# The experts' down product of a routed layer in three f32r passes, with the operand splitting on ScalarE and VectorE

## The reference, cut to what matters

```python
moe = jnp.zeros((B, T, D_MODEL), jnp.float32)
for e in range(N_EXPERTS):                      # 16
    he = jax.nn.silu(h2 @ w_gate[e]) * (h2 @ w_up[e])      # (rows, 256)
    moe = moe + combine[..., e:e + 1] * (he @ w_down[e])   # w_down[e]: (256, 1024)
x = x + moe
y = rmsnorm(x, g_final)
```

## Time and profile before

| what | value |
|---|---|
| median of 3 runs | 482.11 us (481.48 to 494.56) |
| the profiled execution, its time | 483.13 us |
| its span, first to last instruction | 481.3 us |
| PE busy | 439.2 us (91% of the span) |
| DVE busy | 231.1 us (48%) |
| ACT busy | 149.9 us (31%) |
| POOL busy | 112.3 us (23%) |
| mean granted clock of TensorE | 0.957 of full speed |

### The profile page before, as it was taken

How to read it: one execution, slowest core, us unless ns; L and a number is a source line. 1 busy time by engine, 2 the same in 40 slices (tenths; PEclk the granted TensorE clock), 3 DMA queues, 4 the chain that set the end, 5 groups by cost and what they waited for, 6 DMA issues and landing times.

```text
span 481.3 us, 7519 instructions
## 1 busy us (share of the span) xinstructions
PE 439.2 (91%) x2852; PEld 357.7 (74%) x2852; DVE 231.1 (48%) x593; ACT 149.9 (31%) x397; POOL 112.3 (23%) x200
## 2 busy tenths in 40 slices
PE   6999999999899869999997898999999999999950
PEld 3686999988678637888773785888887887878830
DVE  2754234447599866243228354222445555454450
ACT  5475223325477643321113110111221221212230
POOL 2010002000333232100003021222435444454121
PEclk9899999999999959999999798999999999999995
DMA  7851607132000597132206898889999999942100
GB/s 257 266 157 44 208 1 242 32 121 64 1 3 1 192 420 283 42 141 87 82 11 238 330 359 302 334 332 345 337 342 335 342 332 336 327 170 71 63 25 19
DMA packets 32073, 91.39 MB, mean 190 GB/s; under 512 B 11193, under 2 KB 11705, under 8 KB 27942
## 3 DMA queue, kind: packets, MB, share of 16 engines
q1 hardware_dynamic: 20790, 71.97, 41.3%
q0 software_dynamic: 11248, 18.96, 11.3%
HBM read 86.38 MB, written 26.01 MB: 234 GB/s over the span
## 4 chain that ended last, share of the span: by engine, by line
PE 56%; DMA 14%; issue 11%; POOL 7%; DVE 5%; ACT 4%; POOLq 0%; SPq 0%; DVEq 0%; ACTq 0%
PE ps L1075 12%; PE ps L749 9%; PE ps L751 8%; PE ps L750 8%; DMA out_y_sample<-region_x,lists 8%; PE ps L1083 7%; DMA region_x<-h_rows,lists 3%; PE ps L1068 2%; PE ps L870 2%; DMA region_x<-in_x_prompt 1%; POOL region_x L649 1%; PE ps L903 1%; POOL mix L649 1%; POOL out_y_prompt L654 1%; PE ps L958 1%
## 5 line engine op out<-in xcount | busy, mean ns | idle before, releaser
L1075 PEld LDWEIGHTS ps<-region_p,region_a 128*128 128x128 f32 x512 | 58.3, 192 | 3.3 <-issue 3.3
L1075 PE MATMUL ps<-region_p,region_a 128*128 128x128 f32 x512 | 58.5, 275 | 0.0
L751 PE MATMUL ps<-region_a_r,region_w_r 128*128 128x288 f32 x192 | 56.5, 294 | 0.0
L749 PE MATMUL ps<-region_a_r,ring_r 128*128 128x288 f32 x128 | 40.5, 317 | 0.0
L1914 DVE TENSOR_TENSOR region_t<-region_t,ps 128x256 f32<-128x256 f32 x16 | 6.7, 422 | 68.1 <-PE ps L1075 68.1
L750 PE MATMUL ps<-region_a_r,ring_r 128*128 128x288 f32 x128 | 37.7, 295 | 0.0
L1413 ACT ACTIVATE region_t<-ps 128x256 f32<-128x256 f32 x16 | 6.1, 384 | 98.7 <-PE ps L1075 86.5
L649 POOL DMA_INDIRECT region_x<-h_rows,lists x14 | 14.4, 1027 | 93.2 <-DVE slot_w L1909 93.2
L1403 ACT ACTIVATE region_p<-ps,gffn_sb 128x128 f32<-128x128 f32 x64 | 18.3, 368 | 57.1 <-PE ps L1068 57.1
L751 PEld LDWEIGHTS ps<-region_a_r,region_w_r 128*128 128x128 f32 x192 | 36.0, 188 | 0.0
L1075 PEld LDWEIGHTS ps<-region_p,ring 128*128 128x128 f32 x256 | 31.2, 203 | 3.1 <-DVE region_p L1813 1.7
(11 more groups left out here) (309 smaller groups left out, 902.7 us busy)
## 6 DMA issues: line engine op xcount, KB each, us to landing
region_a<-in_w_gate SPq DMA_DIRECT2D x8, 1024.0 KB
region_a<-in_w_up SPq DMA_DIRECT2D x8, 1024.0 KB
region_a<-in_w_down SPq DMA_DIRECT2D x8, 1024.0 KB
region_w<-in_w_in SPq DMA_DIRECT2D x2, 2048.0 KB, 10.3
region_w<-in_w_out SPq DMA_DIRECT2D x2, 2048.0 KB, 8.2
ring<-in_w_gate SPq DMA_DIRECT2D x4, 1024.0 KB
ring<-in_w_up SPq DMA_DIRECT2D x4, 1024.0 KB
ring<-in_w_down SPq DMA_DIRECT2D x4, 1024.0 KB
```

Source lines behind the costliest of these rows:

```text
L749: pe.matmul(out, lhs_hi, rhs_hi, start=first, stop=False)
L751: return pe.matmul(out, lhs_lo, rhs_hi, start=False, stop=last)
L1075: ins = pe.matmul(ps[:, bank, c * P:(c + 1) * P], w[:, k, c * P:(c + 1) * P], xT[:, b, k, :], start=(k == 0), stop=(k == KC - 1))
```

## The change

The down product of every expert in the main pipeline (not in the overflow branch) is split. Per expert i:

- ACT evacuates all eight transposed blocks of expert i + 1, DVE none (except for expert 0). DVE's wait for the transposes goes.
- ACT then writes the high parts of the down weights of expert i + 1, two copies of 128x1024 into `region_q` (float32r), after the weights have landed and the down product that used that half of `region_q` is done.
- DVE subtracts them from the weights in place (`wd_los`, two operations of 128x1024), after `finish` and ahead of the one-hot matrix and `add_rows`.
- `he_out` becomes three DVE operations of 128x256: the high part, the full product again, and the remainder.
- PE runs 12 float32r matmuls of 512 columns in place of 4 float32 ones, and waits for `wd_lo_ready` ahead of them and for `he_lo_ready` after the first four.

```diff
+            def down_split(u, i):
+                b = u % 2
+                for half in range(2):
+                    n = slice(half * 512, (half + 1) * 512)
+                    for c in range(FC):
+                        pe.matmul(ps[:, 4 + half, :], he_hi[:, b, c, :], wd_hi[:, b, c, n], start=(c == 0), stop=False)
+                        pe.matmul(ps[:, 4 + half, :], he_hi[:, b, c, :], wd_lo[u][:, c, n], start=False, stop=False)
+                    if half == 0:
+                        pe.wait_ge(he_lo_ready, i + 1)
+                    for c in range(FC):
+                        ins = pe.matmul(ps[:, 4 + half, :], he_lo[:, b, c, :], wd_hi[:, b, c, n], start=False, stop=(c == FC - 1))
+                    ins.then_inc(down_done, 1)
...
-                pe.wait_ge(xT_dve, i + 1)
+                if first:
+                    pe.wait_ge(xT_dve, 1)
...
-                down(u, b, down_done)
+                pe.wait_ge(wd_lo_ready, i + 1)
+                down_split(u, i)
...
+            def wd_his(i):
+                act.wait_ge(ring_loaded[i % RING], 48 * (i // RING + 1))
+                if i >= 2:
+                    act.wait_ge(down_done, 2 * i - 2)
+                elif i == 0:
+                    act.wait_ge(x2_stored, 16 * NT)
+                    act.wait_ge(h2n_ready, NT)
+                    act.wait_ge(h2_transposed, NT)
+                for c in range(FC):
+                    act.copy(wd_hi[:, i % 2, c, :], wd_sb[i % RING][:, c, :]).then_inc(wd_hi_ready, 1)
...
             ins.then_inc(xT_act, 1)
+            wd_his(0)
...
-                    for k in range(4, KC):
+                    for k in range(KC):
                         ins = rows_out((i + 1) % 2, k)
                     ins.then_inc(xT_act, 1)
+                    wd_his(i + 1)
...
-                dve.tensor_tensor(heT[:, i % 2], gact[:, i % 2],
-                                  ps[:, 3, 0:FE].rearrange("p (c s) -> p c s", c=FC), ALU.mult).then_inc(he_ready, 1)
+                b, up = i % 2, ps[:, 3, 0:FE].rearrange("p (c s) -> p c s", c=FC)
+                dve.tensor_tensor(he_hi[:, b], gact[:, b], up, ALU.mult).then_inc(he_ready, 1)
+                step(dve.tensor_tensor(gact[:, b], gact[:, b], up, ALU.mult))
+                dve.tensor_tensor(he_lo[:, b], gact[:, b], he_hi[:, b].bitcast(F32), ALU.subtract).then_inc(he_lo_ready, 1)
+
+            def wd_los(i):
+                for c in range(FC):
+                    dve.wait_ge(wd_hi_ready, FC * i + c + 1)
+                    ins = dve.tensor_tensor(wd_lo[i % RING][:, c, :], wd_sb[i % RING][:, c, :],
+                                            wd_hi[:, i % 2, c, :].bitcast(F32), ALU.subtract)
+                ins.then_inc(wd_lo_ready, 1)
...
+            wd_los(0)
             for i in range(E - 1):
                 he_out(i)
...
-                dve.wait_ge(xg_transposed, i + 2)
-                rows_out((i + 1) % 2).then_inc(xT_dve, 1)
...
                     finish(i - 1, final_ready)
+                wd_los(i + 1)
                 if i >= 1 and i + 3 < E:
                     expert_onehot(i + 3)
                 add_rows(i)
```

More of the change, by code:

```diff
@@ L135, in build @@
         wd_sb = [r[:, 2 * WB:3 * WB].rearrange("p (c n) -> p c n", c=FC) for r in ring]
-        region_q = sb("region_q", [P, 5632])
+        region_q, region_q_r = sb_both("region_q", [P, 5632])
         qT = region_q[:, 0:2304].rearrange("p (h t) -> p h t", h=H)
@@ L170, in build @@
         xT = region_p[:, :].rearrange("p (b k s) -> p b k s", b=2, k=KC)
-        region_t = sb("region_t", [P, 1536])
+        region_t, region_t_r = sb_both("region_t", [P, 1536])
         aT = region_t[:, 0:1024].rearrange("p (b k) -> p b k", b=2)
@@ L175, in build @@
         heT = region_t[:, 512:1024].rearrange("p (b c s) -> p b c s", b=2, c=FC)
+        he_hi = region_t_r[:, 512:1024].rearrange("p (b c s) -> p b c s", b=2, c=FC)
+        he_lo = region_t_r[:, 1024:1536].rearrange("p (b c s) -> p b c s", b=2, c=FC)
+        wd_hi = region_q_r[:, 0:4 * D].rearrange("p (b c n) -> p b c n", b=2, c=FC)
+        wd_lo = [r.rearrange("p (c n) -> p c n", c=FC) for r in
+                 (ring0_r[:, 2 * WB:3 * WB], region_a_r[:, 2 * WB:3 * WB], region_a_r[:, 5 * WB:6 * WB], region_w_r[:, 2 * WB:3 * WB])]
         region_x, region_x_r = sb_both("region_x", [P, 4096])
@@ L380, in build @@
         he_ready = sem("he_ready")
+        he_lo_ready = sem("he_lo_ready")
+        wd_hi_ready = sem("wd_hi_ready")
+        wd_lo_ready = sem("wd_lo_ready")
         down_done = sem("down_done")
@@ L1084, in down @@
                                         start=(c == 0), stop=(c == FC - 1))
-                    if signal is down_done or half == 1:
-                        ins.then_inc(signal, 1)
+                ins.then_inc(signal, 1)
+            def down_split(u, i):
[10 more added lines that the diff above has]
+                    ins.then_inc(down_done, 1)
             for i in range(2):
@@ L1136, in _ @@
             pe.wait_ge(idx_ready, E + 2)
-            pe.wait_ge(xT_dve, E)
             pe.wait_ge(xT_act, E)
@@ L1401, in rows_out @@
             def rows_out(b, k):
-                return act.activation(xT[:, b, k, :], ps[:, 1, (k - 4) * P:(k - 3) * P], ACT.Copy, scale=gffn_sb[:, k:k + 1])
+                return act.activation(xT[:, b, k, :], ps[:, k // 4, (k % 4) * P:(k % 4 + 1) * P], ACT.Copy, scale=gffn_sb[:, k:k + 1])
+            def wd_his(i):
[8 more added lines that the diff above has]
+                    act.copy(wd_hi[:, i % 2, c, :], wd_sb[i % RING][:, c, :]).then_inc(wd_hi_ready, 1)
             act.wait_ge(h2T_dve, NT)
```

## The result

The changed kernel took 493.31 us in the median of 4 runs (488.22 to 495.18), the kernel before 481.8 us beside it; the ratio is 1.0245, with a 95% interval of 1.0138 to 1.0353. It is slower by some 2.4%, where 0.6% faster was predicted. A second set on another chip gave 493.97 us and 1.0198 (1.013 to 1.0266). Of 14 executions of the kernel before on that chip, ten took 479.2 to 484.3 us and four 490.9 to 494.7, as long as the changed kernel's own eight (488.2 to 499.5), and the ratios compare only the faster group of each kernel.

What follows compares the result with a forecast made beforehand. PE was taken to bound stages A and C, the scatter's round stage B: 483.13 - 3.3 + 1.9 - 1.65 = 480.1 us, stated as 479.6 against the runs' median. The range was 472.5 to 488.

Steps and rivals of the forecast that it cites:

- stage B: Experts' stretch from some 341 to 425 us, DMA near nine tenths busy, chain not through PE; forecast +1.9 us.
- The round: DVE lists, POOL gathers and scatter, landing in y_sample, lists again: some 12.2 us before, against 11.67 us for PE.
- The down product: On PE, per expert: 12 matmuls take 2.77 us in place of 3.54, gain taken as 0.75 us.
- stage A: Experts up to some 341 us, PE full: faster down products gain 3.3 us together, between 2.0 and 3.5.
- ACT, DVE and PE's new waits at no cost: Added evacuations, casts, DVE operations and PE waits fit into idle time, except 0.6 us each at experts 1 and 15.
- The 0.6 us for expert 1: Remainders on DVE delay he_out, so this down product starts about 0.6 us late; expert 15 also loses 0.6 us.
- POOL's block: DVE's weight remainders hold up POOL's scatter to y_prompt: +1.0 us per round, bounds 0 and +2.3.
- Stage C: Experts after 425 us, PE alone decides: three down products gain 2.25 us, less 0.6, so 1.65 us.
- The landing: Scatter to y_sample, issue to landing: later issue shortens it from mean 6.38 to 5.7 us, between 5.04 and 6.38.
- L: Time the scatter to y_sample takes to land: mean 6.38 us before, shortest 5.04, forecast 5.7.
- Rival 2: POOL gets no turn between finish and both remainders, 2.3 us more per round: 484 to 492 us, chance 0.22.
- Rival 1: PE decides in stage B as well, since the landing shortens more or POOL is not blocked: 472.6 us, chance 0.15.

Runs made afterwards that it cites:

- e3: Changed kernel with eight slots of lists in place of four, so lists wait for a scatter four experts earlier: 477.23 us, ratio 0.9865.
- e4: Kernel before with eight slots of lists in place of four: 480.65 us, ratio 0.9956.
- e8: Changed kernel loading only an eighth of the gate and up weights for experts 7 to 15: 468.57 us, ratio 0.9711.
- e6: Kernel before with two unused 128x1024 DVE subtractions per expert after finish, from expert 5 on: 482.66 us, ratio 0.9993, from seven of ten executions.
- e13: Changed kernel with three needless matmuls per expert, PE's period 11.6 us as before: profiled execution 483.53 us, the others 492.78, 499.36 and 500.63.
- e5: Kernel before with one of four down matmuls per expert left out, PE 0.88 us faster per expert, nothing added: 489.9 us, ratio 1.013.
- e2: Changed kernel with the weight remainders on DVE moved behind add_rows: four executions of 496.39, 483.25, 495.8 and 496.05 us.

## Why the prediction was wrong

- **What bounds stage B: right.** The round was on the chain before and after, and cutting it (e3, e4) moved the time by 17 and 2 us.
- **The down product, 0.75 us per expert: right.** The period fell from 11.67 to 11.0 us in stage A and to 10.97 in e8.
- **ACT, DVE and PE's new waits at no cost: right, nearly.** Eight evacuations take 2.2 us, the waits of PE's weight loads for ACT are 0.6 us in all, and PE's for the high part 1.5 us. The 0.6 us for expert 1 did not show (its down product started 1.1 us behind the transposes, as before), nor that for expert 15: DVE was ready for `he_out` 0.19 us before PE was, and the tail from there on was 0.3 us shorter.
- **POOL's block, +1.0 us per round: right in size** (1.98 against 1.02 us), and POOL got its turn behind `finish` every time, as in the earlier trace rows. The inference in the Trainium skill (SBUF — State Buffer, Who interferes with whom), that a `tensor_tensor` does not hold up descriptors, is contradicted by these rows and by those of e6. But by e6 the term costs too little to be told from nothing, since the landing gives most of it back.
- **Stage A, 3.3 us: 2.8.** PE waited 1.06 us for a gather of 9.70 us. **Stage C, 1.65 us: 1.9.**
- **The landing, 5.7 us: this step failed.** It was 8.5 us, 6 x 2.8 = 17 us more than in the sum, and the miss is 15.1 us (495.18 - 480.1): stage B grew by 15.6 us where the sum had 1.9. I read from one kernel that the landings end a fixed time behind the transposes and concluded that a later issue means a shorter landing. The profiled executions of e6 and e13, with the old period of PE and the round in place, agree. It is no rule: in e4, with the round cut, landings end 15 to 20 us behind the start of the transposes, at the same pace of PE. And the change alters the pace, and with it when the loads fly; e5 shows that a faster PE alone gives landings of 7.4 to 11.0 us on the chain (the six of stage B: 5.0 to 11.0, median 8.5). The range's upper bound took L at 6.38 as the worst case, with no reason beyond its having been the mean, although has one of 8.05.
- **Rival 2** named a slower time near the one measured, 492.0, but by a mechanism (no turn for POOL) that did not occur. Rival 1 (PE decides in B as well) did not occur either: it counted DMA's work of 11.1 us a period as DMA's only limit, but the chain waits for the landing of one scatter, also while the engines are half idle.

What stays open is what decides between short and long landings. That loads in flight stretch them is shown (e8); that a short round keeps the scatter in the gap between two experts' loads, and a late one puts rows, sums and scatters all beside the next loads, is only read from the timelines. Nor is it settled whether the added work raises the odds of a long time at PE's old pace (e13: three of four executions at 493 to 501 us; e6: three of ten at 493 to 499). With the round cut, the kernel before had none: all ten of e4 took 477.8 to 481.9 us.

## What to carry to other kernels

Where the chain runs through a transfer's landing, its latency depends on what else is in flight, and a faster engine releases other transfers at other times: before speeding an engine up, cut the wait for the landing, here with twice the slots for lists, and measure the saving on top of that. Test a planned saving by leaving the work out (e5), before building the version that has to pay for it. And a mean latency seen at one pace is no upper bound at another: the range must reach to what a delay of the whole round costs.

## What the runs showed of the hardware

- In stage B, an indirect scatter of one expert's rows to `y_sample` landed in 3.1 (e6) to 12.58 us (e2) from issue, with all loads in place, and in 3.0 to 5.2 us with 7/8 of the gate and up loads left out (e8). In the changed kernel the two shortest, 5.72 and 6.63 us, had a DMA share of 0.64 and 0.51, the three longest 0.93 to 0.95.
- POOL's indirect DMA was held up by DVE operations with two SBUF inputs and went on when the one instruction ended (in the rows from 359.48 to 365.12, the gather of the sums and the scatter to `y_prompt` end 0.9 us behind the DVE instruction that held them), also between two that followed each other on DVE. The scatter to `y_prompt` is issued just as the first half of the remainders ends, and waits for the second: 1.97 to 1.99 us in place of 1.02 in every round of stage B, in the changed kernel and in e6.
- After PE had waited 3.53 us for rows, its granted clock was 0.50 from 365.83 to 371.33 us, the level of 1.2 GHz, and the matmuls of the first half of the down product started 0.43 us apart in place of 0.23. PE was not on the chain there.
